# Two transformer blocks on one core: dense weight chunks, tokens and contexts stored as one 16 KB piece per partition

## The reference

```python
mod = silu_c @ w_mod[layer] + b_mod[layer]
h = modulate(rms_norm(x, norm1_w[layer]), sh1, sc1)
q, k, v, g, f = split_proj(h @ wi)
x = x + g1 * y
x = x + g2 * conv_ffn(h2, w_up[layer], conv_w[layer], conv_b[layer], w_down[layer])
```

```python
g = jnp.einsum('becd,edf->becf', xe, w_gate)
u = jnp.einsum('becd,edf->becf', xe, w_up)
y = jnp.einsum('becf,efd->becd', jax.nn.silu(g) * u, w_down)
```

## Time and profile before

| | us |
|---|---|
| median of 3 runs | 2445.08 |
| lowest and highest run | 2440.34, 2445.99 |
| profiled execution, first to last instruction | 2436.4 |
| median less that span: what lies around it | 8.7 |
| TensorE busy in that span | 2297.3 (94%) |

### The profile page before, as it was taken

The page is one execution under the profiler, slowest core; times in us unless marked ns, Lnnn a source line. Parts: engine busy times, 40 slices in busy tenths (PEclk is TensorE's granted clock), DMA queues, the critical chain, the costliest instruction groups (busy, mean ns, idle before and its releaser), DMA issues.

```text
span 2436.4 us, 25813 instructions
## 1 busy us (share of the span) xinstructions
PE 2297.3 (94%) x11168; PEld 1505.0 (62%) x11168; DVE 918.2 (38%) x1196; ACT 621.3 (26%) x883; POOL 152.9 (6%) x138
## 2 busy tenths in 40 slices
PE   6999999999999999999999997998899989898998
PEld 4874878877888888886678885434343434343433
DVE  4937454555578524596642433010000000000001
ACT  5315323244233335516543221000000000000001
POOL 0222000110000011040000020000000000000000
PEclk8999999999999999999999998999999999999999
DMA  7220344344564323220012236999999999999997
GB/s 275 104 81 1 143 149 141 136 139 152 193 207 173 139 104 106 102 78 36 1 35 95 78 139 270 420 429 427 428 426 429 427 428 427 428 428 427 428 426 303
DMA packets 114215, 570.04 MB, mean 234 GB/s; under 512 B 5726, under 2 KB 28679, under 8 KB 87991
## 3 DMA queue, kind: packets, MB, share of 16 engines
q1 hardware_dynamic: 98224, 523.51, 53.2%
q0 software_dynamic: 7152, 27.99, 3.2%
q10 hardware_dynamic: 8727, 16.91, 2.0%
HBM read 566.28 MB, written 2.10 MB: 233 GB/s over the span
## 4 chain that ended last, share of the span: by engine, by line
PE 36%; DMA 17%; DVE 3%; ACT 1%; issue 1%; SPq 0%; DVEq 0%; ACTq 0%
PE ps L1362 9%; PE ps L811 9%; DMA arena<-in_w_exp_up 8%; PE ps L1462 6%; DMA arena<-in_w_exp_gate 4%; DMA weights<-in_w_exp_gate 3%; PE ps L1341 3%; DVE arena L2141 1%; PE ps L1237 1%; PE ps L1217 1%; DMA weights<-in_w_exp_up 1%; PE ps L1382 1%; DMA weights<-in_w_exp_down 1%; PE ps L1175 1%; PE ps L1194 1%
## 5 line engine op out<-in xcount | busy, mean ns | idle before, releaser
L811 PE MATMUL ps<-weights_r 128*128 128x512 f32 (+1 forms) x2784 | 855.4, 387 | 9.0 <-DVE hT_r L2059 5.9
L811 PEld LDWEIGHTS ps<-weights_r 128*128 128x128 f32 x2784 | 520.1, 188 | 119.0 <-issue 13.6
L811 PE MATMUL ps<-hT_r,weights_r 128*128 128x512 f32 x1264 | 462.4, 390 | 0.0
L1362 PE MATMUL ps<-weights,arena 128*64 128x512 f32 x768 | 351.6, 614 | 57.4 <-DMA weights<-in_w_exp_up 44.6
L1364 PE MATMUL ps<-weights,arena 128*64 128x512 f32 x768 | 352.3, 615 | 0.0
L1362 PEld LDWEIGHTS ps<-weights,arena 128*64 128x64 f32 x768 | 105.6, 141 | 283.7 <-issue 282.4
L2040 DVE TENSOR_TENSOR weights_r<-weights,weights_r 128x4096 fp32r<-128x4096 f32 (+1 forms) x46 | 197.1, 4285 | 202.4 <-ACT weights_r L1547 200.6
L811 PEld LDWEIGHTS ps<-hT_r,weights_r 128*128 128x128 f32 x1264 | 238.2, 188 | 49.2 <-issue 0.5
L811 PE MATMUL ps<-arena_r,weights_r 128*128 128x512 f32 (+1 forms) x640 | 224.4, 387 | 0.0
L1547 ACT ACTIVATE weights_r<-weights 128x4096 fp32r<-128x4096 f32 (+1 forms) x46 | 161.6, 3514 | 216.8 <-PE ps L811 116.0
L2658 DVE TENSOR_TENSOR hT<-hT,ps 128x512 f32<-128x512 f32 x32 | 22.0, 688 | 450.9 <-PE ps L1364 450.9
(11 more groups left out here) (308 smaller groups left out, 2467.7 us busy)
## 6 DMA issues: line engine op xcount, KB each, us to landing
weights<-in_w_exp_gate SPq DMA_DIRECT2D x48, 2048.0 KB, 23.0
weights<-in_w_exp_down SPq DMA_DIRECT2D x42, 2048.0 KB, 27.7
weights<-in_w_exp_up SPq DMA_DIRECT2D x42, 2048.0 KB, 26.2
weights<-in_w_in SPq DMA_DIRECT2D x18, 2048.0 KB, 7.9
arena<-in_w_exp_gate SPq DMA_DIRECT2D x16, 2048.0 KB, 27.0
arena<-in_w_exp_down SPq DMA_DIRECT2D x14, 2048.0 KB, 27.5
arena<-in_w_exp_up SPq DMA_DIRECT2D x14, 2048.0 KB, 27.5
weights<-in_w_up SPq DMA_DIRECT2D x22, 1024.0 KB, 7.8
```

The lines of the kernel that those rows point to most:

```text
L811: last = pe.matmul(t, a if w_first else b, b if w_first else a, start=(k == 0 and n == 0), stop=(k == kt - 1 and n == len(pairs) - 1))
L1362: la = pe.matmul(bank(b0 + n)[0:64, :], xe[:, 2 * j + r, 0:64], wa[:, r, n * 512:(n + 1) * 512], start=start, stop=stop)
```

## The change

The host stores `x`, both contexts and `w_down` with a partition's rows side by side, and every other dense matrix chunk by chunk, with the eight pieces of a partition side by side. `w_up` gets the two halves of its chunk side by side first, so that one load of 2 MB takes the place of two of 1 MB. What lands in the weight buffers is the same as before, number by number. The expert weights, the small loads, all products and all waits stay as they are.

```diff
-        def kmaj(w, n0, n1):
-            return w[:, n0:n1].rearrange("(k p) n -> p k n", p=P)
+        def columns(w, n0):
+            return w[n0 // 512]
...
-        early = {"x": (3, x[0].rearrange("(t p) d -> p t d", p=P)),
-                 ("mod1", 2): (5, kmaj(w_mod[0], 1024, 1536)),
-                 "ctx": (4, ctx[0].rearrange("(t p) d -> p t d", p=P))}
+        early = {"x": (3, x),
+                 ("mod1", 2): (5, columns(w_mod, 1024)),
+                 "ctx": (4, ctx)}
...
         for j in range(UPN):
-            chunk(("up", j), kmaj(w_up[0], 256 * j, 256 * j + 256),
-                  kmaj(w_up[0], FFN + 256 * j, FFN + 256 * j + 256))
+            chunk(("up", j), w_up[j])
...
-            part = w_down[0][512 * j:min(512 * j + 512, FFN), :].rearrange("(k p) n -> p k n", p=P)
+            part = w_down[:, 4 * j:min(4 * j + 4, FT), :]
...
+def rows_by_partition(a):
+    return np.ascontiguousarray(a.reshape(-1, P, a.shape[-1]).swapaxes(0, 1))
+
+def chunks_of_columns(w):
+    w = w[0].reshape(w.shape[1] // P, P, w.shape[2] // 512, 512)
+    return np.ascontiguousarray(w.transpose(2, 1, 0, 3))
+
+BY_COLUMNS = ["w_mod", "w_in", "w_four_out", "w_ret_out", "w_branch_gate", "w_out", "w_up", "w_ada_2",
+              "w_in_2", "w_proj_a_2", "w_proj_b_2", "w_out_2"]
+BY_ROWS = ["x", "ctx", "ctx_2", "w_down"]
...
+    up = tensors["w_up"].reshape(1, D, 2, UPN, 256).swapaxes(2, 3)
+    tensors["w_up"] = up.reshape(1, D, 2 * FFN)
+    for name in BY_COLUMNS:
+        tensors[name] = chunks_of_columns(tensors[name])
+    for name in BY_ROWS:
+        tensors[name] = rows_by_partition(tensors[name])
```

More of the change, by code:

```diff
@@ L398, in chunk @@
             chunks.append(parts)
-        early = {"x": (3, x[0].rearrange("(t p) d -> p t d", p=P)),
-                 ("mod1", 2): (5, kmaj(w_mod[0], 1024, 1536)),
-                 "ctx": (4, ctx[0].rearrange("(t p) d -> p t d", p=P))}
+        early = {"x": (3, x),
+                 ("mod1", 2): (5, columns(w_mod, 1024)),
+                 "ctx": (4, ctx)}
         def mod1(i):
-            chunk(("mod1", i), kmaj(w_mod[0], 512 * i, 512 * i + 512))
+            chunk(("mod1", i), columns(w_mod, 512 * i))
         def in1(i):
-            chunk(("in1", i), kmaj(w_in[0], 512 * i, 512 * i + 512))
+            chunk(("in1", i), columns(w_in, 512 * i))
         mod1(0)
@@ L421, in build_two_blocks @@
                     ("proj", "a"): (w_four_out, 0), ("proj", "b"): (w_ret_out, 0)}[kind, part]
-            chunk(("m1", kind, part, nq), kmaj(w[0], o + 512 * nq, o + 512 * nq + 512))
+            chunk(("m1", kind, part, nq), columns(w, o + 512 * nq))
             if kind == "gate":
@@ L425, in mod2 @@
         def mod2(i):
-            chunk(("mod2", i), kmaj(w_ada_2[0], 512 * i, 512 * i + 512))
+            chunk(("mod2", i), columns(w_ada_2, 512 * i))
         for nq in range(2):
-            chunk(("out1", nq), kmaj(w_out[0], 512 * nq, 512 * nq + 512))
+            chunk(("out1", nq), columns(w_out, 512 * nq))
             mod1(10 + nq)
         for j in range(UPN):
-            chunk(("up", j), kmaj(w_up[0], 256 * j, 256 * j + 256),
-                  kmaj(w_up[0], FFN + 256 * j, FFN + 256 * j + 256))
+            chunk(("up", j), w_up[j])
             mod2(j)
         for j in range(6):
-            part = w_down[0][512 * j:min(512 * j + 512, FFN), :].rearrange("(k p) n -> p k n", p=P)
+            part = w_down[:, 4 * j:min(4 * j + 4, FT), :]
             if j < 5:
@@ L441, in build_two_blocks @@
             else:
-                chunk(("down", j), part, ctx_2[0].rearrange("(t p) d -> p t d", p=P))
+                chunk(("down", j), part, ctx_2)
         for i in range(7):
-            chunk(("in2", i), kmaj(w_in_2[0], 512 * i, 512 * i + 512))
+            chunk(("in2", i), columns(w_in_2, 512 * i))
         for kind, part, nq in MERGE:
@@ L447, in build_two_blocks @@
                     ("proj", "a"): (w_proj_a_2, 0), ("proj", "b"): (w_proj_b_2, 0)}[kind, part]
-            chunk(("m2", kind, part, nq), kmaj(w[0], o + 512 * nq, o + 512 * nq + 512))
+            chunk(("m2", kind, part, nq), columns(w, o + 512 * nq))
         for nq in range(2):
-            chunk(("out2", nq), kmaj(w_out_2[0], 512 * nq, 512 * nq + 512))
+            chunk(("out2", nq), columns(w_out_2, 512 * nq))
         NCH = len(chunks)
@@ L719, in _ @@
                 src = chunks[n]
[L720 to L730, removed]
+                o = 0
+                for part in src:
+                    k, w = part.shape[1], part.shape[2]
+                    sp.dma_start(slots[sl][:, o:o + k * w].rearrange("p (k n) -> p k n", k=k),
+                                 part).then_inc(S[f"landed{sl}"], 16)
+                    o += k * w
                 if order[n] == ("in1", 0):
```

## The result

The changed kernel takes 2454.88 us (median of 4 runs, 2452.95 to 2456.70) against 2443.66 us before (4 runs beside it, 2440.34 to 2445.99): 1.0046 times as long, 95% interval 1.0032 to 1.0060. It is slower by 11.2 us (interval 8 to 15 us). The prediction gave 2447 us, no change that can be told, with a range of 2439 to 2457 us; its rival 1, late vectors, gave 2456 us.

What follows compares the result with a forecast made beforehand. The prediction took TensorE to bound the dense stages and transfers the expert stage; 2436.4 - 1.8 + 4.1 = 2438.7 us of span, plus 8.7 us between span and run median, gave 2447 us, range 2439 to 2457 us.

Steps and rivals of the forecast that it cites:

- rival 1: Start: TensorE's first instruction waits until each small-load signal takes its own 16 KB turn; 25.4 us, +11.3 us, 2456 us; chance 0.27.
- The loss at the start: TensorE's first instruction, waiting for 15 small vector loads beside 16 KB pieces, comes at 16.4 instead of 12.3 us: 4.1 us lost.
- If a signal goes along with its row: Small loads at the start: only 21 rows take turns of 0.64 us from 3 us on, so vectors land at 16.4 us.
- the upper bound of that step: Small loads at the start: signals take a turn each, 35 turns, vectors at 25.4 us, a loss of 13.1 us.
- the central forecast: Whole kernel: no change that can be told, within 0.3% (7.3 us); chance 0.60.
- the value in between: Start: the 4.1 us loss, chosen between a gain of 3.1 us and a loss of 13.1 us.
- The gain of 1.8 us: Start: TensorE's 1.8 us wait for `w_mod` chunk 3 goes in full, since it lands at 33.4 us, wanted at 36.3 us.
- Dense stages 0: Dense stages, 61 to 1480 us: TensorE's work covers faster loads, so no change; at most 1 us gain, no loss.
- signs of being wrong: First dense to first expert product changing by over 2 us, or the first wait staying at 12 us.
- Rival 2: Start: a load's whole share takes one turn, 4.9 us; vectors land when SP's queue runs dry, 27.5 us; 2458.5 us; chance 0.06.
- Rival 3: Start: small loads land early, at 9.2 us, and the clock stays up; -7.4 us, 2438 us; chance 0.13.
- Rival 4: Dense loads: the pieces are cut again, so engines move 2 or 4 KB as before; 2445 us; chance 0.04.

Runs made afterwards that it cites:

- packed kernels: All 18 small vectors packed on the host into one array, loaded at once: in the changed kernel 2439.65 us, in the kernel before 2443.06 us.

## Why the prediction was right, and which step of it failed

**The place and the mechanism were right.** The experts and the dense stages kept their length within what single profiles differ by, and what moved was TensorE's first instruction, held by small loads that take turns with 16 KB pieces.

**The loss at the start was mis-sized.** The step that failed is "If a signal goes along with its row, 21 rows are left: 3 + 21 x 0.64 = 16.4 us". Signals take turns of their own, as the two runs with 40 more rows show, and the upper bound of that step, 35 turns and 25.4 us, was the measured value, 25.6 us. So rival 1, at 0.27, was the case that came, with 2456 us against 2454.9, and the central forecast, no change that can be told, at 0.60, was not. 2454.9 us lies within the range because the range took in rival 1. I chose the value in between although I wrote that q10's rows fit both ends equally. They didn't settle it: the rows at 8 to 11 us come from a queue that, as the runs with 1 KB pieces and with x alone show, was held by something else than turns, and nothing about a 16 KB turn could be read from them. Only the count of packets, 407, was safe, and with the eight engines assumed it spoke for 37 small packets on each. That rival 1's 11.3 us stand so near the measured 11.2 is in part luck: in the profiles the first dense product came 13.5 us later, since of the gain of 1.8 nothing was left.

**The gain of 1.8 us** was right in that the wait for `w_mod` 3 went. It shows nowhere in the time: the vectors' delay took it along, and the clock took as much. These are the products with `w_mod` 1 and 2 in the new kernel (start us, us):

```profile
39.63 3.64 PE L912 MATMUL ps<-weights,sc_pad 128*32 128x512 f32 x16
...
45.79 3.64 PE L912 MATMUL ps<-weights,sc_pad 128*32 128x512 f32 x16
```

Chunk 2 took 1.92 us before and takes 3.64 us, in a stretch from 37.8 to 54.9 us at 0.50 of the full clock, the 1.2 GHz level, where before it was a shorter one. That is 1.7 us against the gain of 1.8. It is the largest of several small shifts and not the whole account: TensorE also waits 1.8 us before its first dense product, for DVE's rounding, which it didn't before, and its turning of the context just ahead took 1.9 us instead of 3.4. From the first turning of vectors to the first dense product the two profiles need 47.8 - 12.4 = 35.4 and 61.3 - 25.6 = 35.7 us.

**Dense stages 0**: right as to the layout, and shown by the two runs that move only the first five loads. But one of the prediction's own signs of being wrong did come up: from the first dense to the first expert product it allowed 2 us, and the stretch grew by 3.3. The sign was set too tight. With only the first five loads in new pieces the same stretch grew by 4.8 us (57.5 to 1517.0 us), and with all dense weights changed but the first five by 1.7 (48.8 to 1505.2). Single profiles of these kernels differ by more than 2 us there whatever the layout. ACT's waits for `w_up`, which should have gone, did not:

```profile
ACT weights_r L1541 <- DMA weights<-in_w_down: 21.4, 1, 21.4
ACT weights_r L1541 <- DMA weights<-in_w_up: 20.1, 4, 5.6
```

They were 22.0 and 24.1 us. The new layout took 0.6 us off the first and 4.0 off the second, and TensorE did not wait behind them either time.

**Rival 2**, a whole load in a turn, is out: the small packets go one for one with single pieces, and the vectors landed at 25 us, before the queue ran dry. What the Trainium skill says in "DMA: Bandwidth & Descriptors", section "Queues, rings and completion order", of typically 9 to 17 descriptors drained from a queue before the next, is not how these engines treated 16 KB pieces: 11 pieces went with 12 small packets. **Rival 3**, early vectors, would have needed x out of the way: they land at 8.0 us only with nothing beside them, and at 12.2 us with x alone in 16 KB pieces. **Rival 4**: the pieces did not get cut again; at 17 to 24 us q1's 2.88 MB in 198 packets are nearly all of 16 KB.

## What to carry to other kernels

Before making a transfer's pieces longer, look for what shares the engines with it. Beside pieces of 16 KB, small loads that somebody waits for paid about one piece for every row and for every signal on their busiest engines, so count their packets and multiply; that is good to some 2 us (25.4 us for 25.6 with 16 KB, 14.5 for 16.7 with 8 KB), and does not hold for pieces of 4 KB and less. Pack small vectors into one load before lengthening the others: here the long pieces cost 11 us without that, and were worth 3.4 us with it. Where TensorE's own work covers the loads, as in these dense stages, faster ones were worth nothing that the runs could tell, though they were 73 of the 78.

## What the runs showed of the hardware that was not expected

**A single load does not land sooner in long pieces.** From issue to landing, a load of `w_in` in the kernel before, and in the changed one (times issued, KB, median us):

```profile
weights<-in_w_in SPq DMA_DIRECT2D x18, 2048.0 KB, 7.9
```

```profile
weights<-in_w_in SPq DMA_DIRECT2D x18, 2048.0 KB, 8.1
```

A queue that is full moves 425 GB/s in pieces of 16 KB and 388 in 2 KB, but in the median landing time of these loads, most of them issued one at a time in the dense stages, the gain doesn't show. It showed where loads stand in a queue: at the start of the packed kernels, `w_mod` 2 was there at 30.0 us in the new layout and at 32.4 in the old.

**Back to back, loads in short pieces hold SP, in long ones they don't.** Issuing two `w_mod` loads took SP 4.67 us in pieces of 2 KB, 9.24 us in pieces of 1 KB, and 0.91 us in pieces of 16 KB. It is not the pieces alone: x, just before and in 512 pieces, took 0.42 us, and the next chunk of `w_in`, issued at 31.25 us in pieces of 2 KB, 0.64 us. What SP waits for no run shows. The row of the run with 1 KB:

```profile
1.66 9.24 SPq L729 DMA_DIRECT2D weights<-in_w_mod  x2
```
